# Two heads at a time in the neighbourhood and axial attention of a four-layer fp32 block

## The reference, cut to what matters

```python
def global_axial_attention(q, k, v, gq, gk):      # 8 query heads of 64, 2 key/value heads, 512 keys
    ...                                           # rmsnorm and 2-D rotary on q and k, q * 64 ** -0.5
    s = jnp.einsum('bqkgd,bskd->bkgqs', qi, k).astype(jnp.float32)
    p = jax.nn.softmax(s, axis=-1)
    return jnp.einsum('bkgqs,bskd->bqkgd', p.astype(v.dtype), v)

def neighbourhood_attention(q, k, v, rpb):        # 8 heads of 64, an 8 x 64 grid, 16 columns of neighbours
    s = jnp.einsum('bqhd,brqjhd->bhqrj', q_row, k_nb).astype(jnp.float32)
    s = s + bias.astype(jnp.float32)[None]
    p = jax.nn.softmax(s.reshape(...), axis=-1)
    return jnp.einsum('bhqrj,brqjhd->bqhd', p, v_nb)
```

## Time and profile before

| | us |
|---|---|
| median of 3 runs | 3582.84 (3582.16 to 3588.26) |
| the profiled execution | 3583.34 |
| its span | 3581.5 |

### The profile page before, as it was taken

One profiled execution on the slowest core, in us unless ns is written; L12 is line 12 of the kernel. 1 busy time (PEld: TensorE's weight loads), 2 busy tenths in 40 slices (PEclk: granted clock), 3 DMA queues, 4 the chain that ended last, 5 costly groups with the idle time before them and its releaser, 6 DMA issues.

```text
span 3581.5 us, 41808 instructions
## 1 busy us (share of the span) xinstructions
PE 3422.0 (96%) x16765; PEld 2753.0 (77%) x16765; DVE 1806.4 (50%) x2360; ACT 1225.4 (34%) x1664; POOL 139.1 (4%) x148
## 2 busy tenths in 40 slices
PE   7999999999999999999999998999989999999999
PEld 6565788888885657888888756888878888878887
DVE  3555445555245554455553895555244344365543
ACT  2424323444234242234432424343222122244432
POOL 1102000000011110000000001000000000000000
PEclk9998999999998989999999998999989999999999
DMA  5210222222241102322233111222221212223222
GB/s 154 45 45 24 70 94 94 94 95 99 100 104 33 57 12 73 103 94 94 94 100 100 59 47 65 94 94 100 98 74 59 94 59 70 83 71 100 94 94 83
DMA packets 231695, 288.16 MB, mean 80 GB/s; under 512 B 5396, under 2 KB 188716, under 8 KB 231564
## 3 DMA queue, kind: packets, MB, share of 16 engines
q1 hardware_dynamic: 225628, 266.89, 22.5%
q0 software_dynamic: 5936, 19.40, 2.5%
HBM read 284.18 MB, written 2.10 MB: 80 GB/s over the span
## 4 chain that ended last, share of the span: by engine, by line
PE 90%; DVE 6%; ACT 2%; issue 1%; POOL 0%; DMA 0%; DVEq 0%; POOLq 0%; ACTq 0%
PE ps L1340 17%; PE ps L1341 17%; PE ps L1342 17%; PE ps L1437 6%; PE ps L1438 6%; PE ps L1439 6%; PE ps L1513 4%; PE ps L1492 3%; PE ps L1609 2%; PE ps L1373 2%; PE ps L1375 2%; PE ps L1374 2%; PE ps L1545 2%; PE ps L1656 1%; ACT t_whi L569 1%
## 5 line engine op out<-in xcount | busy, mean ns | idle before, releaser
L867 DVE TENSOR_TENSOR t_wlo<-t_wraw,t_whi 128x2048 fp32r<-128x2048 f32 x252 | 579.1, 2298 | 1325.5 <-ACT t_whi L569 1325.5
L1340 PE MATMUL ps<-t_hh,t_whi 128*128 128x512 f32 (+1 forms) x2624 | 984.2, 375 | 45.4 <-DVE t_hl L937 27.1
L569 ACT ACTIVATE t_whi<-t_wraw 128x2048 fp32r<-128x2048 f32 x252 | 482.7, 1916 | 1475.3 <-PE ps L1342 983.3
L1341 PE MATMUL ps<-t_hl,t_whi 128*128 128x512 f32 (+1 forms) x2624 | 976.1, 372 | 0.0
L1342 PE MATMUL ps<-t_hh,t_wlo 128*128 128x512 f32 (+1 forms) x2624 | 976.0, 372 | 0.0
L1340 PEld LDWEIGHTS ps<-t_hh,t_whi 128*128 128x128 f32 x2624 | 501.3, 191 | 137.5 <-issue 22.6
L1341 PEld LDWEIGHTS ps<-t_hl,t_whi 128*128 128x128 f32 x2624 | 501.1, 191 | 85.6 <-issue 2.5
L1342 PEld LDWEIGHTS ps<-t_hh,t_wlo 128*128 128x128 f32 x2624 | 501.0, 191 | 83.3
L1439 PE MATMUL ps<-t_whi,t_midl 128*128 128x512 f32 x704 | 273.9, 389 | 0.0
L1437 PE MATMUL ps<-t_whi,t_midh 128*128 128x512 f32 x704 | 273.9, 389 | 0.0
L1438 PE MATMUL ps<-t_wlo,t_midh 128*128 128x512 f32 x704 | 273.9, 389 | 0.0
(11 more groups left out here) (244 smaller groups left out, 4206.6 us busy)
## 6 DMA issues: line engine op xcount, KB each, us to landing
t_wraw<-in_w_in_dram SPq DMA_DIRECT2D x46, 1024.0 KB, 5.1
t_wraw<-in_w_up_dram SPq DMA_DIRECT2D x44, 1024.0 KB, 5.0
t_wraw<-in_ffn_w_in_dram SPq DMA_DIRECT2D x44, 1024.0 KB, 5.0
t_wraw<-in_w_kv_dram SPq DMA_DIRECT2D x24, 1024.0 KB, 5.1
t_wraw<-in_w_down_dram SPq DMA_DIRECT2D x20, 1024.0 KB, 4.9
t_wraw<-in_ffn_w_out_dram SPq DMA_DIRECT2D x20, 1024.0 KB, 4.9
t_wraw<-in_w_branch_dram SPq DMA_DIRECT2D x12, 1024.0 KB, 4.9
t_wraw<-in_w_q_dram SPq DMA_DIRECT2D x12, 1024.0 KB, 5.0
```

Of the source, the lines that this page charges most:

```text
L569: sc.activation(whi[slot][:, :], wraw[slot][:, :], ACT.Copy).then_inc(w_hi, 1)
L867: v.tensor_tensor(wlo[slot][:, :], wraw[slot][:, :], whi[slot][:, :].bitcast(F32), ALU.subtract).then_inc(w_lo, 1)
L1340: te.matmul(out, wh, xh, start=first, stop=False)
L1341: te.matmul(out, wh, xl, start=False, stop=False)
```

## The change

Steps go pair by pair: for each pair of heads and block of queries, both heads follow each other. TensorE gets a loop of its own for C and A, over 16 pairs of steps: scores of the next pair (two matmuls back to back, on partition rows 0 to 63 and 64 to 127, into two banks), transposes of the pair's first step, values of the pair before (for each of the four key blocks, head one and then head two, on other columns), transposes of the second step. Scores use banks 0, 1 and 6, 7 in turn, and the pooled matmuls go to banks 5 and 4. The turned probabilities get four buffers instead of two. ScalarE and VectorE get loops to match. Attention D keeps its order.

```diff
-POOL_STEPS = (16, 20, 24, 28)
+POOL_PAIRS = (3, 7, 11, 15)

...
-            return [(2 * hp + s, b) for hp in range(4) for s in range(2) for b in range(4)]
+            return [(2 * hp + s, b) for hp in range(4) for b in range(4) for s in range(2)]
+        def score_bank(n):
+            return bank(6 * (n // 2 % 2) + n % 2)
+        def turned_probs(g):
+            return gain[:, (g % 4) * T:(g % 4 + 1) * T]
...
+            def pair_attention(kind, n0, pbuf, extra):
+                def exp(n):
+                    g = n0 + n
+                    s, q = g % SLOTS, g % 4
+                    act.wait_ge(maxed, g + 1)
+                    if n >= SLOTS:
+                        act.wait_ge(turned, g - SLOTS + 1)
+                    p = pbuf[:, s * T:(s + 1) * T]
+                    sc.activation(p, p if kind == "C" else score_bank(n), ACT.Exp, bias=small[:, q:q + 1],
+                                  scale={"A": 0.125, "C": 1.0}[kind], accum_out=small[:, 8 + q:9 + q]).then_inc(probs, 1)
+                def copy(n):
+                    act.wait_ge(turned, n0 + n + 1)
+                    if n >= 4:
+                        act.wait_ge(weighted, n0 + 2 * (n // 2) - 2)
+                    sc.activation(turned_probs(n0 + n), bank(2 + n % 2), ACT.Copy).then_inc(pt_ready, 1)
+                exp(0)
+                exp(1)
+                if 0 in extra:
+                    extra[0]()
+                for j in range(18):
+                    if 1 <= j <= 16:
+                        copy(2 * j - 1)
+                    if j >= 5 and (j - 5) % 4 == 0:
+                        y_round(n0, (j - 5) // 4, 8 if kind == "C" else 0)
+                    if j < 16:
+                        copy(2 * j)
+                    if j < 15:
+                        exp(2 * j + 2)
+                        exp(2 * j + 3)
+                    if j and j in extra:
+                        extra[j]()
             def y_round(n0, hp, t0):
...
+            def pair_attention(n0, pbuf, scores_in, scale, pair_out, extra):
+                negated_max(n0, 0, scores_in, scale)
+                negated_max(n0, 1, scores_in, scale)
+                divide(n0, pbuf, T)
+                for j in range(18):
+                    if j < 16:
+                        divide(n0 + 2 * j + 1, pbuf, T)
+                    if j == 0 and j in extra:
+                        extra[j]()
+                    if j < 15:
+                        negated_max(n0, 2 * j + 2, scores_in, scale)
+                        negated_max(n0, 2 * j + 3, scores_in, scale)
+                        divide(n0 + 2 * j + 2, pbuf, T)
+                    if j and j in extra:
+                        extra[j]()
+                    if j >= 5 and (j - 5) % 4 == 0:
+                        pair_out((j - 5) // 4)
...
-                    src = bank((2, 6, 4, 6)[j - 2], 2) if j >= 2 else None
+                    src = bank((2, 4, 6, 4)[j - 2], 2) if j >= 2 else None

...
+            def turn_probs(n0, n, pbuf):
+                g = n0 + n
+                pe.wait_ge(scaled, g + 1)
+                if n >= 2:
+                    pe.wait_ge(pt_ready, g - 1)
+                for j in range(4):
+                    at = (g % SLOTS) * T + j * P
+                    ins = te.transpose(bank(2 + n % 2)[:, j * P:(j + 1) * P], pbuf[:, at:at + P], ident)
+                ins.then_inc(turned, 1)
+            def pair_attention(kind, n0, scores, pbuf, weigh, v_drained=None, behind=None, extra={}):
+                for j in range(17):
+                    if j < 15:
+                        if j:
+                            pe.wait_ge(probs if kind == "A" else maxed, n0 + 2 * j)
+                        scores(j + 1)
+                    if j < 16:
+                        turn_probs(n0, 2 * j, pbuf)
+                    if j in extra:
+                        extra[j]()
+                    if j == 16 and behind:
+                        behind()
+                    if j == 1 and v_drained:
+                        pe.wait_ge(drained, v_drained)
+                    if j:
+                        pe.wait_ge(pt_ready, n0 + 2 * j)
+                        weigh(j - 1)
+                    if j < 16:
+                        turn_probs(n0, 2 * j + 1, pbuf)
             def weigh_pair(kind, l, vbuf):
-                def weigh(n, g):
-                    h, b = steps_of(kind)[n]
-                    hp, r = h // 2, 64 * (h % 2)
-                    if n % 8 == 0 and hp >= 2:
+                def weigh(j):
+                    hp, b = divmod(j, 4)
+                    if b == 0 and kind == "A" and hp:
+                        pe.wait_ge(pool_lo, 4 * l + hp)
+                    if b == 0 and hp >= 2:
                         pe.wait_ge(y_lo, PAIRS[f"{kind}{l}"] + hp - 1)
                     for k in range(4):
-                        at = k * 512 + h * 64 if kind == "C" else k * P + 64 * (h // 4)
-                        ins = te.matmul(bank(4 + hp % 2)[r:r + 64, b * P:(b + 1) * P], vbuf[:, at:at + 64],
-                                        scratch[:, (g % 2) * T + k * P:(g % 2) * T + (k + 1) * P], start=k == 0, stop=k == 3)
-                    ins.then_inc(weighted, 1)
+                        for s in range(2):
+                            r, h = 64 * s, 2 * hp + s
+                            at = k * 512 + h * 64 if kind == "C" else k * P + 64 * (h // 4)
+                            ins = te.matmul(bank(4 + hp % 2)[r:r + 64, b * P:(b + 1) * P], vbuf[:, at:at + 64],
+                                            turned_probs(2 * j + s)[:, k * P:(k + 1) * P], start=k == 0, stop=k == 3)
+                    ins.then_inc(weighted, 2)
                 return weigh
...
                         ins.then_inc(init_turn, 1)
                 for j in range(2, 5):
                     start(c + j, d=d + j)
-                    if j == 3 and l == 0:
+                    if j == 4 and l == 0:
                         pe.wait_ge(init_out, 3)
                     if j < 4:
-                        rows_out(c + j, (hh, hl), bank0=(2, 6)[j - 2]).then_inc(w_used, 1)
+                        rows_out(c + j, (hh, hl), bank0=(2, 4)[j - 2]).then_inc(w_used, 1)
                     else:
-                        tokens_out(c + j, (hh, hl), 0, CW, 4).then_inc(w_used, 1)
-
-                def scores_c(n, g):
-                    h, b = steps_of("C")[n]
-                    r, t = 64 * (h % 2), h // 2
-                    te.matmul(bank(g % 2), qC[r:r + 64, t * T + b * P:t * T + (b + 1) * P], kC[r:r + 64, t * T:(t + 1) * T],
-                              start=True, stop=True).then_inc(scored, 1)
+                        tokens_out(c + j, (hh, hl), 0, CW, 6).then_inc(w_used, 1)
+                def scores_c(j):
+                    t, b = divmod(j, 4)
+                    for s in range(2):
+                        r = 64 * s
+                        te.matmul(score_bank(2 * j + s), qC[r:r + 64, t * T + b * P:t * T + (b + 1) * P],
+                                  kC[r:r + 64, t * T:(t + 1) * T], start=True, stop=True).then_inc(scored, 1)
                 pe.wait_ge(drained, 2 + d + 4)
-                for n in range(2):
-                    scores_c(n, STEPS[f"C{l}"] + n)
+                scores_c(0)
                 start(c + 5, d=d + 5)
-                tokens_out(c + 5, (hh, hl), 0, CW, 6).then_inc(w_used, 1)
+                tokens_out(c + 5, (hh, hl), 0, CW, 4).then_inc(w_used, 1)
+                pe.wait_ge(drained, 2 + d + 5)
                 def first_a(c=FIRST[f"a_qkv{l}"], d=DRAINS[f"a_qkv{l}"]):
                     start(c, d=d)
                     rows_out(c, (hh, hl), bank0=0).then_inc(w_used, 1)
-                attention("C", STEPS[f"C{l}"], 32, scores_c, pC, weigh_pair("C", l, vC), v_drained=2 + d + 6, behind=first_a)
+                pair_attention("C", STEPS[f"C{l}"], scores_c, pC, weigh_pair("C", l, vC), v_drained=2 + d + 6, behind=first_a)
                 def head_mean(t, l=l):
...
                 pe.wait_ge(qk_ready, 6 * l + 6)
                 pe.wait_ge(drained, 2 + d + 2)
-                def scores_a(n, g):
-                    h, b = steps_of("A")[n]
-                    r, t, kv = 64 * (h % 2), h // 2, int(h % 2 != h // 4)
-                    te.matmul(bank(g % 2), qA[r:r + 64, t * T + b * P:t * T + (b + 1) * P], kA[r:r + 64, kv * T:(kv + 1) * T],
-                              start=True, stop=True).then_inc(scored, 1)
+                def scores_a(j):
+                    t, b = divmod(j, 4)
+                    for s in range(2):
+                        r, kv = 64 * s, int(s != t // 2)
+                        te.matmul(score_bank(2 * j + s), qA[r:r + 64, t * T + b * P:t * T + (b + 1) * P],
+                                  kA[r:r + 64, kv * T:(kv + 1) * T], start=True, stop=True).then_inc(scored, 1)
                 def pooled_out(g, l=l):
                     W = T + 2 * PAD
                     pe.wait_ge(pooled, 4 * l + g + 1)
-                    if g >= 2:
```

(42 more changed lines are left out.)

58 lines of the change are left out of this document (27 added, 31 removed).

## The result

The changed kernel takes 3458.58 us (median of 4 runs, 3458.04 to 3461.24) against 3582.5 us. The ratio is 0.9648, with a 95% interval of 0.9633 to 0.9663: 124 us less. The forecast was 92 us less, and 3491 us; the measured time lies at the lower edge of the range, where rival 3 stood (3457 us, chance 0.07). The profiled execution took 3458.37 us.

What follows compares the result with a forecast made beforehand. TensorE was taken as the bound; shorter pairs (3.79 us against 5.32) save 98 us, less 3 for C's starts, 1 for mask additions, 2 for A's ends: 92 us less, 3491 us, range 3458 to 3570.

Steps and rivals of the forecast that it cites:

- rival 3: In pairs of C and A, both heads run fully abreast; 3457 us, or 3467 if VectorE ends up bounding; chance 0.07.
- the three slots for scores: Scores of a pair's two heads in C and A overlap partly, taking three record times, 1.48 us.
- the nine for values: Values of a pair's two heads in C and A overlap, sixteen records in nine record times, 1.13 us.
- the lower end of both bounds: Fully abreast times per pair on TensorE: scores 1.05 us, values 1.02 us.
- the order of issue: Objection to full overlap: TensorE issues in order, head one's two score records and then head two's.
- rivals 1, 2 and 4: No overlap, 3567 us, 0.12; only scores 3540 or values 3519 us, 0.15; head changes cost like shape changes, 3647 us, 0.13.
- the start of C: TensorE waits for a division, resuming about 111.1; net idle 3.8 instead of 2.25 us, 3 us more in two stages.
- The end of A: Last values wait some 0.8 us for the copy of the last transposes; 2 us in two stages.
- 1 us more for both stages: TensorE's stalls behind GpSimd's four mask additions in C cost about 1 us more through reduced slack.
- The bound for the ring: Per pair, transposes, copy, exponential, division and next transposes across three engines take 2.9 to 3.1 us, below 3.79.

Runs made afterwards that it cites:

- x2: Changed kernel with a pair's values ordered head one's key blocks 0 to 3, then head two's; 3479.52 us.
- x4: Changed kernel with values ordered head one blocks 0, 1, head two blocks 0, 1, then blocks 2, 3 of each likewise; 3459.41 us.
- x13: Changed kernel with values ordered head one blocks 0 to 2, head two blocks 0 to 2, then block 3 of each; 3469.71 us.
- x3: Changed kernel with both scores of a pair on rows 0 to 63 and values head by head; 3525.42 us.
- x6: Changed kernel with both transposes of a pair together before the values, three changes of shape instead of four; 3460.91 us.
- x1: Changed kernel with both scores of a pair on rows 0 to 63; 3503.9 us.
- x5: Changed kernel with values still alternating, but both heads writing columns 0 to 63 as one accumulation; 3496.98 us.
- x14: Changed kernel with GpSimd adding C's mask to only one of 28 rows of the bias; 3444.37 us.
- x15: Changed kernel with GpSimd adding C's mask to one of 28 rows and both transposes of a pair before the values; 3446.11 us.
- x9: Changed kernel with both transposes of a pair before the values and the division in C and A covering 8 of 512 columns; 3450.38 us.

## Why the prediction was wrong

**The step that failed** is the sentence "The second record of a head needs the same rows as its first, so head two can start only beside head one's second record", and with it the three slots for scores and the nine for values. Its first half holds. The second took the list for a queue that a waiting record blocks. The runs showed a look past three waiting records (x2, x4, x13), so with two records of one head in front nothing is lost. Scores take 2 slots, 1.06 us for 1.48, and values 8, 1.02 for 1.13. That is 0.42 + 0.11 = 0.53 us a pair, 64 x 0.53 = 34 us, against the 32 us by which forecast and result differ (92 and 124). That these agree to 2 us is in part luck, for the rest of the sum was off both ways: TensorE's busy time fell by 141 us where 64 x 2.07 is 132, and its idle time grew by 16 us where the forecast had 6. I had the right number as the lower end of both bounds, and priced it as rival 3 at 3457 us. Its objection, "the order of issue", had no row behind it. Between two ends with no row nearer to one of them, 0.07 was too little.

**What held.** TensorE was the bound and stayed so (x3). The gaps belong to changes of shape: a pair's transposes still take 0.59 us in both places, and x6 takes one gap away and its good pairs shrink from 3.26 to 3.10 us. The scores and the values both overlap, each by its own half of rows or columns (x1, x5); rivals 1, 2 and 4 fall. Of the rules weighed, the one that weight loads overlap only with another row group (the Trainium skill, TensorE: Matmul & The Clock Gate, Part 3) does not hold for these loads of 64 columns: sixteen fit in 0.85 us under matmuls on the same rows. The same part of that page of the Trainium skill says that matmuls start and end strictly in list order. Here head two's first record begins 0.53 us before head one's second, and in x2 the eight records of each head, 0.87 us in a line, are over in 1.51 us, with head two's first record ahead of head one's last three. So "the engines run each its own instruction list in order" is not exact for TensorE either: it holds for matmuls on the same rows and columns (x1, x5).

**The small terms.** At the start of C TensorE resumes at 111.29 us (forecast 111.1):

```profile
105.41 1.13 PE L1633 MATMUL ps<-t_kC,t_qC 64*128 64x512 f32 x4
111.29 1.12 PE L1564 MATMUL ps<-t_base,t_pC 128*128 128x128 f32 x4 [4.75 <-DVE t_pC L1013]
```

The idle time is 4.75 instead of 3.8 us, since the two pairs of scores before it are shorter by 0.42 us each. (The 3.8 does not come out of the step it is given with: 2.25 + 2.3 - 1.48 is 3.1. It comes out if two pairs of scores of 1.48 us replace two single ones of 1.05: 2.25 + 2.3 - 0.86 = 3.7.) The end of A waits 0.69 us for the copy (forecast 0.8):

```profile
1230.82 1.09 PE L1600 MATMUL ps<-t_gain,t_vA 128*64 128x128 f32 x16 [0.69 <-ACT t_gain L695]
```

TensorE's waits for divisions in C, the waits view of C0 and C1 after:

```profile
PE ps L1564 <- DVE t_pC L1013: 9.6, 4, 4.8
```
```profile
PE ps L1564 <- DVE t_pC L1013: 12.3, 6, 4.8
```

Without the 4.8 us at each start that is 4.8 and 7.5 us, against 4.8 and 2.8 before (the stall of the earlier trace rows is part of the first). I had put 1 us more for both stages and it is 5. x14 shows that these waits hang on the mask additions: without them the waits behind the start shrink to 1 us a stage. With a pair of 3.26 us VectorE has little room to catch up after one; I had checked it against 3.79. The bound for the ring, 2.9 to 3.1 us, was low as well: x15 shows 3.24.

A term that the forecast did not have is TensorE's wait for divisions in A, 3.0 and 3.8 us after and nothing before. All but 1 us of each lies at the start of the stage, where GpSimd works on the pooled mixer and divisions take 1.1 to 1.6 us instead of 0.49.

## What to carry to other kernels

Matmuls of half the rows or half the columns are worth pairing: two took the time of one, for scores and for values. The partner may stand a few records behind in the list: for the values four cost 0.05 us, six 0.27; for the scores only two were tried. Count the changes between 64 rows, 64 columns and the full array, at 0.15 to 0.19 us each, and look afterwards at the engine that had slack before: here VectorE went from 60% to 85% of C0, and the next microseconds lay in GpSimd's long instructions and not on TensorE.

## What the runs showed of the hardware that was not expected

- TensorE looks past three waiting records: 2, 4, 6, 8 records of one half in front of the other's gave 1.02, 1.07, 1.29, 1.51 us for sixteen.
- A VectorE division in SBUF beside a GpSimd addition took up to 4.07 us (0.49 alone), and one of 8 columns 3.91 (0.23 alone, x9), each ending within 0.3 us of the addition's end. Cutting the addition in seven brought the mean in C0 from 0.69 to 0.56 us; in fourteen, the addition grew to over 6 us and the total was less good again (3455 us for 3451).
- A wait of 3.36 us was followed by matmuls at the 1.2 GHz level in x9's C1; waits of 1.04 and 1.29 us in its C0 were not.
